# The same tuned decoder block with the inverse's substitution spread behind the attention maxima, and the halves of its second level alternated on TensorE

## What is computed

```python
kkT = jnp.einsum('nbhid,nbhjd->nbhij', k_beta, k)
A = jnp.eye(C, dtype=jnp.float32) + jnp.where(strict, kkT * decay, 0.0)
rhs = jnp.concatenate([v_beta, k_beta * jnp.exp(g)[..., None]], axis=-1)
sol = lax.linalg.triangular_solve(A, rhs, left_side=True, lower=True, unit_diagonal=True)
...
_, o = lax.scan(step, s0, (q, k, u, w, g, attn_intra))
```

```python
probs = jax.nn.softmax(logits, axis=-1)
w = probs[:, :, 0] - lam * probs[:, :, 1]
return jnp.einsum('bhqk,bkhe->bqhe', w.astype(v.dtype), v)
```

## Time and profile before

| what | value |
|---|---|
| time, median of 3 runs (lowest to highest) | 1159.39 us (1157.6 to 1159.72) |
| the profiled execution: time, span | 1160.82 us, 1159.0 us |
| busy: PE, PEld | 1123.9 us (97%), 898.7 us (78%) |
| busy: DVE, ACT, POOL | 655.2, 549.4, 633.1 us |
| the chain that ended last | PE 87%, DVE 9%, ACT 3% |
| mean granted clock of TensorE | 0.995 |

### The profile page before, as it was taken

The page is one execution under the profiler, slowest core; times in us unless marked ns, Lnnn a source line. Parts: engine busy times, 40 slices in busy tenths (PEclk is TensorE's granted clock), DMA queues, the critical chain, the costliest instruction groups (busy, mean ns, idle before and its releaser), DMA issues.

```text
span 1159.0 us, 16765 instructions
## 1 busy us (share of the span) xinstructions
PE 1123.9 (97%) x5502; PEld 898.7 (78%) x5502; DVE 655.2 (57%) x1036; ACT 549.4 (47%) x886; POOL 633.1 (55%) x769
## 2 busy tenths in 40 slices
PE   6998989999999999999999999999999999999997
PEld 4786667777777777667878888888888888888886
DVE  4668976767666776862213324476776515731534
ACT  5584647566565656551322124544444314433542
POOL 6386264546554564645456554566576754573452
PEclk9999999999999999999999999999999999999999
DMA  8354031331404123213223523333333432332232
GB/s 243 77 132 130 26 94 35 85 85 35 102 18 118 38 64 100 75 54 85 79 77 105 181 72 91 91 93 114 103 90 91 116 102 73 109 96 80 74 89 79
DMA packets 196619, 104.36 MB, mean 90 GB/s; under 512 B 3926, under 2 KB 195401, under 8 KB 196553
## 3 DMA queue, kind: packets, MB, share of 16 engines
q1 hardware_dynamic: 196172, 103.39, 32.0%
q10 hardware_dynamic: 381, 0.15, 0.1%
HBM read 101.40 MB, written 2.13 MB: 89 GB/s over the span
## 4 chain that ended last, share of the span: by engine, by line
PE 87%; DVE 9%; ACT 3%; issue 1%; ACTq 0%; DVEq 0%
PE bank L562 75%; PE bank L698 2%; PE bank L712 1%; DVE prod L1810 1%; DVE xs L1812 1%; PE bank L705 1%; PE bank L657 1%; DVE pr L1722 1%; PE bank L922 1%; DVE pr L1721 0%; DVE oa_lo L1978 0%; PE bank L909 0%; PE bank L919 0%; PE bank L910 0%; PE bank L913 0%
## 5 line engine op out<-in xcount | busy, mean ns | idle before, releaser
L492 POOL TENSOR_TENSOR w_lo<-w_raw,w_hi 128x256 fp32r<-128x256 f32 x692 | 549.9, 828 | 259.9 <-ACT w_hi L1074 254.2
L562 PE MATMUL bank<-hn_hi,w_hi 128*128 128x512 f32 x1000 | 408.4, 408 | 1.0 <-DVE o_a L1985 1.0
L562 PE MATMUL bank<-hn_hi,w_lo 128*128 128x512 f32 x1000 | 391.0, 391 | 0.0
L562 PE MATMUL bank<-hn_lo,w_hi 128*128 128x512 f32 x1000 | 390.4, 390 | 0.0
L562 PEld LDWEIGHTS bank<-hn_hi,w_hi 128*128 128x128 f32 x1000 | 189.0, 189 | 43.7 <-issue 9.2
L562 PEld LDWEIGHTS bank<-hn_hi,w_lo 128*128 128x128 f32 x1000 | 187.9, 188 | 40.4
L562 PEld LDWEIGHTS bank<-hn_lo,w_hi 128*128 128x128 f32 x1000 | 188.7, 189 | 34.6 <-issue 1.7
L507 POOL CAST w_hi<-w_raw 128x1024 fp32r<-128x1024 f32 x70 | 78.2, 1117 | 222.0 <-PE bank L562 131.3
L1074 ACT ACTIVATE w_hi<-w_raw 128x1024 fp32r<-128x1024 f32 x111 | 117.9, 1062 | 77.6 <-PE bank L562 69.7
L2096 DVE SCALAR_TENSOR_TENSOR u<-vr,pt,u 128x511 f32<-128x511 f32 x88 | 88.9, 1010 | 8.3 <-DVE u L2096 0.7
L2090 DVE TENSOR_TENSOR vr<-bank,rs 128x512 f32<-128x512 f32 x44 | 30.4, 692 | 72.5 <-PE bank L562 67.1
(11 more groups left out here) (308 smaller groups left out, 1643.6 us busy)
## 6 DMA issues: line engine op xcount, KB each, us to landing
w_raw<-in_w_in SPq DMA_DIRECT2D x73, 512.0 KB, 6.7
w_raw<-in_w_up SPq DMA_DIRECT2D x44, 512.0 KB, 3.8
w_raw<-in_w_down SPq DMA_DIRECT2D x16, 512.0 KB, 3.9
crow<-cum_rows_out SPq DMA_DIRECT2D x16, 256.0 KB, 5.7
w_raw<-in_w_br_a SPq DMA_DIRECT2D x8, 512.0 KB, 4.0
w_raw<-in_w_br_b SPq DMA_DIRECT2D x8, 512.0 KB, 4.0
w_raw<-in_w_out SPq DMA_DIRECT2D x8, 512.0 KB, 3.9
w_raw<-in_w_ple_gate SPq DMA_DIRECT2D x8, 512.0 KB, 4.0
```

The source lines that it names most:

```text
L492: ins = pool.tensor_tensor(wlo[c.slot][:, ks, :], raw[c.slot][:, ks, :], whi[c.slot][:, ks, :].bitcast(F32), ALU.subtract)
L562: mm = pe.matmul(acc, w[c.slot][:, i, :], xx[:, x0 + i, :], start=(i == 0 and n == 0), stop=last)
```

## The change

VectorE: `prep(0, 1)` moves ahead of the scaling of `li`; in the lead fewer columns of the substitution stand ahead of each `combine`; `prep(1, 1)` stands behind column 24 and not 28; columns 26 to 31 and both transposes move into turn 0, between that turn's first two quarters of the attention, with the second transpose behind `maxima(1, 1)`. The products `at_`, `qeg` and `vbt` of turn 0 come later. ScalarE: its pieces of both levels move back to fit. TensorE: one step more stands ahead of `scores(0, 0)`; in turn 0 `pair_low` moves behind `scores(1, 1)` and three steps, everything of the levels behind it moves back too, and the halves are issued as one group, `halves(g)`, in which a lower half of group g + 1 and an upper half of group g take turns. GpSimd's and SyncE's lists are unchanged.

```diff
-STEPS_FIRST = ((2, 4, 1, 9, 1, 8, 1, 8), ((1, 1), (1, 1, 1), (1, 1, 1), (1, 1, 1)))
+STEPS_FIRST = ((2, 4, 1, 8, 1, 8, 1, 9), ((1, 1), (1, 1, 1), (1, 1, 1), (1, 1, 1)))
...
+            def halves(g):
+                pe.wait_ge(sem("placed"), 2 if g < 0 else 6)
+                pe.wait_ge(sem("pairs"), 1 if g < 1 else 2)
+                if g >= 0:
+                    pe.wait_ge(sem("inverse_ui"), g + 3)
...
                 for n in range(8):
-                    m = g * 8 + n
...
+                    if g < H // 2 - 1:
+                        low = low_half(8 * g + 8 + n)
+                    if g >= 0:
+                        high = high_half(8 * g + n)
...
             def lead_turn(at, fill):
-                f.step(1)
+                f.step(2)
                 scores(0, 0)
...
-                f.step(before[1] - 2 if h == 0 else before[1])
+                f.step(before[1])
...
-                if h == 0:
-                    for g in range(2):
-                        pair_low(g)
-                        f.step(1)
                 if attention:
                     turn_w(a, 0)
                 f.step(before[2])
                 if attention:
                     scores(a, 1)
+                if h == 0:
+                    f.step(3)
+                    pair_low(0)
+                    f.step(1)
+                    pair_low(1)
+                    f.step(2)
...
-                if h < H // 2:
-                    half_low(h)
-                f.step(before[5])
+                if 0 < h < H // 2:
+                    halves(h)
+                if h == 0:
+                    f.step(1)
+                    pair_high(0)
+                    f.step(2)
+                    pair_high(1)
+                    f.step(before[5] - 3)
...
+                if h == 0:
+                    f.step(3)
+                    halves(-1)
+                    f.step(3)
+                    halves(0)
+                    f.step(before[7] - 6)
...
 # VectorE, the end of lead_turn
-                substitute(18, 24)
+                substitute(14, 20)
                 steps(finish_silu(0, 2))
                 attention_scale(0)
-                substitute(24, 28)
+                substitute(20, 24)
+                prep(1, 1)
                 first_mask()
-                prep(1, 1)
-                substitute(28, 31)
-                turn_back()
+                substitute(24, 26)
...
 # VectorE, turn 0
+                if h == 0:
+                    maxima(a, 0)
+                    substitute(26, 28)
+                    combine(a, 0)
+                    substitute(28, 31)
+                    turn_back()
+                    maxima(a, 1)
+                    turn_again()
+                    scaled_keys()
+                    combine(a, 1)
+                    scaled_values()
```

More of the change, by code:

```diff
@@ L868, in turn @@
                 mm.then_inc(sem("vb_T"), 1)
-                if h == 0:
-                    f.step(before[3] - 5)
-                    pair_high(0)
-                    f.step(2)
-                    pair_high(1)
-                    f.step(3)
-                else:
-                    f.step(before[3])
+                f.step(before[3] - 6 if h == 0 else before[3])
                 if attention:
@@ L892, in turn @@
                     scores(a, 3)
-                f.step(before[7])
+                if h == 0:
[4 more added lines that the diff above has]
+                    f.step(before[7] - 6)
+                else:
+                    f.step(before[7])
                 if more_a:
@@ L1405, in turn @@
                     softmax(a, 3)
+                    if h == 0:
+                        half_copy(1)
+                        half_take(0)
                     silu_exp(a, 2)
@@ L1882, in turn @@
                 a = h + 1
-                if attention:
-                    maxima(a, 0)
-                if h > 0 and halves_ob(h - 1):
-                    low_ob(h - 1)
-                dve.wait_ge(sem("qk"), h + 1)
-                dve.wait_ge(sem("dec"), h + 1)
-                done(V.tensor_tensor(flat(at_), bank[6][:, :], flat(dec), ALU.mult), "qk_read", h + 1)
-                dve.wait_ge(sem("eg"), h + 1)
-                done(V.tensor_tensor(flat(qeg), qb[:, :], flat(eg), ALU.mult), "qeg", h + 1)
@@ L1892, in turn @@
-                if attention:
-                    combine(a, 0)
-                else:
-                    low_a(range(5, 7))
-                if h > 0:
-                    key_decays(h)
-                if attention:
-                    maxima(a, 1)
-                    if h > 0:
-                        finish_ob(h - 1)
-                else:
-                    low_a(range(7, H))
-                dve.wait_ge(sem("vb_T"), h + 1)
-                done(V.tensor_tensor(vbt[:, :, :], tiles(6), kroot[:, h * NT:(h + 1) * NT].unsqueeze(2).to_broadcast([P, NT, P]),
-                                     ALU.mult), "turned_read", h + 1)
@@ new lines, in turn @@
+                if h == 0:
+                    maxima(a, 0)
[8 more added lines that the diff above has]
+                    scaled_values()
+                else:
+                    if attention:
+                        maxima(a, 0)
+                    if halves_ob(h - 1):
+                        low_ob(h - 1)
+                    scaled_keys()
+                    if attention:
+                        combine(a, 0)
+                    else:
+                        low_a(range(5, 7))
+                    key_decays(h)
+                    if attention:
+                        maxima(a, 1)
+                        finish_ob(h - 1)
+                    else:
+                        low_a(range(7, H))
+                    scaled_values()
+                    if attention:
+                        combine(a, 1)
@@ L1909, in turn @@
+                if attention:
+                    steps(conv(a, 0, at("qb")))
+                    maxima(a, 2)
+                    steps(finish_silu(a, 0))
+                    combine(a, 2)
                     if h == 0:
@@ L1912, in turn @@
                         key_decays(h)
-                    steps(conv(a, 0, at("qb")))
-                    maxima(a, 2)
-                    steps(finish_silu(a, 0))
-                    combine(a, 2)
                     steps(conv(a, 2, at("vb")))
```

89 lines of the change are left out of this document (48 added, 41 removed).

## The result

The changed kernel took 1167.9 us (median of seven runs, 1163.2 to 1168.6) beside 1159.0 us before: a ratio of 1.0071, with a 95% interval from 1.0056 to 1.0087. It is slower by 0.7%, and 6.5 us above the forecast of 1161.4 us, outside its range. Two later sets of the same kernel gave 1165.5 and 1166.7 us (ratios 1.0051 and 1.0055); the sixteen times together have a median of 1166.4 us. The profiled execution took 1168.64 us.

What follows compares the result with a forecast made beforehand. TensorE, busy 97% of the span, bounds the kernel. Its standing or slow time goes from 9.0 to 14.7 us (+5.7), the halves return 3.7: 1159.4 + 2.0 = 1161.4 us, range 1158.8 to 1165.3 us.

Steps and rivals of the forecast that it cites:

- The halves: Turns 1 to 3: three mixed groups each cost what one kind costs, saving 3 times 1.23, 3.7 us.
- The rival without overlap: Mixed halves in turns 1 to 3 don't run side by side: they give 0.5 us, total 1164.6 us; chance 0.15.
- The waits of the lead: Lead and turn 0's start: 1.09 and 1.51 us go, 1.82 becomes 0.3, the keys' 0.83 becomes 1.5 us.
- stand against operations that ran slowly there beside GpSimd: VectorE's few new waits for scores in the lead are offset by formerly slow operations: no new gaps booked.
- The stall: Turn 0's ninth step: TensorE waits for the second weight chunk from 154.5 to 165.7 us, 11.2 us (9.5 to 12.5).
- The clock behind the stall: After the chunk's wait in turn 0, half clock costs 1.7 us again, bounds 0 and 3.4 us.
- a second 1.7 us: Thin `pair_low` products behind the restart keep the clock low: total 1163.1 us; chance 0.20, shared with 2 us more waits.
- By position: Check at turn 0's scan: its first product moves from 191.39 to 197.0 us, +5.6 us.
- The sign: Whole kernel: slower by more than 0.2% given 0.20 + 0.15 + 0.15, faster 0.08.
- five waits of before: TensorE's old waits in the lead and turn 0: 1.09, 1.82, 1.51, 0.83 and 2.09 us, together 7.34 us.
- same: Whole kernel: time within 0.2%, 2.3 us, of before; chance 0.30 + 0.05 + 0.07.

## Why the prediction was wrong

**The halves: right.** Booked -3.7 us. In the trace a mixed group takes 1.08 us against 1.07 us for one kind; alone they gave -3.0 us (-1.9 to -4.2). The rival without overlap falls.

**The waits of the lead: right in the large, with 1.2 us not seen.** Booked 0.3 us and 1.5 us; the trace has 0.18 and 1.52. Not booked: 0.87 us at 115.52 and 0.28 us at 123.45. The text took it that VectorE's new waits "stand against operations that ran slowly there beside GpSimd". They did not cover it: the operation that TensorE waits for there was slow before (1.30 us from 116.42 us, beside a cast from 116.41 us) and was slow again. VectorE, then GpSimd, in the profiled execution of the first set:

```profile
114.32 1.14 DVE L1739 SCALAR_TENSOR_TENSOR pr<-pr,ast 128x256 f32<-128x256 f32 x1
```

```profile
114.11 1.07 POOL L507 CAST w_hi<-w_raw 128x1024 fp32r<-128x1024 f32 x1 [2.84 <-PE bank L562]
```

And in the third set's, where TensorE did not wait there:

```profile
113.20 0.48 DVE L1739 SCALAR_TENSOR_TENSOR pr<-pr,ast 128x256 f32<-128x256 f32 x1
```

```profile
113.54 1.05 POOL L507 CAST w_hi<-w_raw 128x1024 fp32r<-128x1024 f32 x1 [2.70 <-PE bank L562]
```

The same operation takes 1.14 us when GpSimd's cast has begun 0.2 us earlier, and 0.48 us when the cast begins 0.3 us later. By the Trainium skill ("SBUF — State Buffer", "SBUF: two separate sides") VectorE with two inputs from SBUF and GpSimd share one pair of ports, and who comes first holds it for its whole instruction. The rows fit in the main: of the two it is the later one that is long. They don't fit to the end: held for the whole cast, until 115.18 us, and with 0.48 us of its own, the operation would have ended at 115.66 us, and it ended at 114.32 + 1.14 = 115.46 us (GpSimd's spans are rough).

**The stall: right.** Booked 11.2 us (9.5 to 12.5), measured 11.51. TensorE ran dry at 156.0 instead of 154.5 us, the chunk came at 167.5 instead of 165.7 us: both ends 1.5 to 1.8 us late, by 1.15 us of the waits above and a start of the lead that was 0.5 us later (VectorE's first `qa` at 94.15 us, before at 93.61). The chain of reasons (GpSimd's list, the second transpose, who stands behind) was as told.

**The clock behind the stall: this step failed.** "A wait of 11 us leaves no reason for less, so I book 1.7 us again", with bounds of 0 and 3.4 us. The three traces of the changed kernel lost 5.8, 2.0 and 6.5 us. The row that the price was taken from the earlier trace rows was a wait of 2.09 us with dense steps behind it, and nothing in the rows said that a stall of 11 us costs the same. Dense steps behind a long stall cost 2.9 to 3.0 us in the runs; the thin products, which the text had as a rival with "a second 1.7 us", cost up to 3.5 us on top. The mechanism of that rival was right, its size was half of what it can be, and with two of three traces beyond even that, its chance of 0.20 was too small.

**By position.** The scan's first product came at 202.89 us, not at 197.0: 5.9 us late. Of these, the waits are 14.36 - 13.0 = 1.4 us, the clock is 5.8 - 1.7 = 4.1 us, and the later start 0.5 us: 6.0 us. In the second set's trace it came at 198.43 us; there the clock is 0.3 us from what was booked, and the whole execution took 1164.3 us, inside the range. That is in part luck: its lead had begun at 92.91 us, 1.2 us earlier than in the first set's. The turns behind it are as before but for the halves: the span grew by 7.9 us, 3.6 us less than the 11.5 us by which the scan is late.

**The sign** was the likeliest one, with too little on it. It was right that the chunk's stall outweighs all five waits of before. With the clock term between 2.0 and 6.5 us there was nothing left of "same".

## What to carry to other kernels

When work is moved ahead of other work, list every engine that waits for what is now later, the one that feeds weights too: here VectorE's second transpose, 3.6 us later by the count, stood ahead of a weight chunk in GpSimd's in-order list, and cost more than all the waits it was moved for. Price a stall with what stands behind it, by a range: dense work behind it paid some 3 us for the clock, thin products 2 to 6.5 us, so put the thin products into the stall or well behind the restart. When two kinds of small products can overlap, issue them in turns, one by one. And before a difference of 3 us is explained by a trace, look at a second trace of the same program; one execution's stretch of half clock is not the program's.

## What the runs showed of the hardware

- Behind one and the same stall of 11.5 us and the same products, the clock was back after 4.0 us in one execution and after 11.6 and 13.0 us in two others.
- The clock does not fall as soon as the engine stands still: in the changed kernel the last product ended at about 156.0 us, and the stretch from 158 to 160 us still has a mean of 0.65. Most of what is at half clock inside the stall costs nothing; only what is left at the restart does. A mean clock over a run counts both.
- Products of 64x64 on opposite quarters of the array overlap fully when they alternate: 32 in 1.08 us against 16 in 1.07 us. The same 32 in two runs of 16, one kind behind the other, take 1.82 us.
